# The feed-forward down projection as a two-by-two block product with seven block products, its sums made by VectorE

## What is computed

```python
gate = causal_dwconv(h @ w_gate, conv_w) + conv_b
return (jax.nn.silu(gate) * (h @ w_up)) @ w_down      # (256 x 5632) @ (5632 x 2048)
...
x = x + g2 * conv_ffn(h, ffn_w_gate[l], ffn_w_up[l], ffn_conv_w[l], ffn_conv_b[l], ffn_w_down[l])
```

## Time and profile before

| | |
|---|---|
| median of 3 runs | 3437.06 us (3432.53 to 3437.33) |
| the profiled execution's own time | 3433.15 us |
| its span, first to last instruction | 3431.5 us |
| mean granted TensorE clock | 0.913 |
| TensorE matmuls busy | 2862.7 us, 83% |
| VectorE busy | 1491.9 us, 43% |
| ScalarE busy | 453.9 us, 13% |
| HBM read | 918.41 MB, 270 GB/s over the span |

### The profile page before, as it was taken

One profiled execution on the slowest core, in us unless ns is written; L12 is line 12 of the kernel. 1 busy time (PEld: TensorE's weight loads), 2 busy tenths in 40 slices (PEclk: granted clock), 3 DMA queues, 4 the chain that ended last, 5 costly groups with the idle time before them and its releaser, 6 DMA issues.

```text
span 3431.5 us, 25630 instructions
## 1 busy us (share of the span) xinstructions
PE 2862.7 (83%) x9302; PEld 1698.2 (49%) x9302; DVE 1491.9 (43%) x2221; ACT 453.9 (13%) x1049; POOL 938.2 (27%) x713
## 2 busy tenths in 40 slices
PE   5999877989999999999999997677776666666666
PEld 3443656578888885444447746233332222222222
DVE  5665265122300000000205407665667776767765
ACT  1000233021010100000205501000010111000000
POOL 2111100000000000000002204655556566665563
PEclk9999978899999999999999998888898888888888
DMA  9999320346544444444631147999999999999998
GB/s 379 395 401 363 116 90 35 123 160 245 207 147 155 151 150 144 147 159 147 210 124 53 39 159 304 419 388 417 390 403 422 422 421 411 418 422 422 421 422 357
DMA packets 232376, 922.74 MB, mean 269 GB/s; under 512 B 17820, under 2 KB 37476, under 8 KB 160356
## 3 DMA queue, kind: packets, MB, share of 16 engines
q0 software_dynamic: 99840, 637.57, 45.3%
q1 hardware_dynamic: 132181, 283.96, 24.1%
q10 hardware_dynamic: 272, 0.13, 0.0%
HBM read 918.41 MB, written 8.44 MB: 270 GB/s over the span
## 4 chain that ended last, share of the span: by engine, by line
PE 56%; DMA 24%; DVE 10%; POOL 5%; issue 3%; ACT 2%; POOLq 0%; DVEq 0%; SPq 0%; ACTq 0%
PE ps L1278 18%; PE ps L966 11%; DMA arena<-in_peer_v,proj 11%; PE ps L1304 9%; PE ps L1515 6%; DMA proj<-in_peer_v,proj 4%; DMA proj<-in_peer_u,proj 4%; DMA ring<-in_w_in 3%; PE ps L1087 3%; DMA arena<-in_w_mod 2%; POOL arena L520 2%; PE ps L1492 2%; PE ps L1004 2%; POOL proj L520 1%; DVE proj L2122 1%
## 5 line engine op out<-in xcount | busy, mean ns | idle before, releaser
L1515 PE MATMUL ps<-proj,gates 128*128 128x512 f32 x992 | 574.2, 743 | 383.9 <-DMA proj<-in_peer_v,proj 272.3
L1278 PE MATMUL ps<-hT,ring 128*128 128x256 f32 x2816 | 608.2, 379 | 1.5 <-ACT hT L559 1.5
L1515 PEld LDWEIGHTS ps<-proj,gates 128*128 128x128 f32 x992 | 233.2, 243 | 721.4 <-issue 602.1
L1278 PEld LDWEIGHTS ps<-hT,ring 128*128 128x128 f32 x2816 | 535.0, 190 | 74.8 <-issue 2.2
L966 PE MATMUL ps<-ring,hT 128*128 128x512 f32 (+2 forms) x960 | 382.8, 559 | 8.0 <-DMA ring<-in_w_in 7.9
L2122 DVE CUSTOM_DVE_ANT_0 arena<-arena,yT 128x2048 f32<-128x2048 f32 x128 | 291.5, 2291 | 211.1 <-DMA arena<-in_peer_u,proj 210.6
L2122 DVE CUSTOM_DVE_ANT_0 proj<-proj,yT 128x2048 f32<-128x2048 f32 x128 | 292.1, 2292 | 121.5 <-DMA proj<-in_peer_u,proj 117.8
L1304 PE MATMUL ps<-ring,arena 128*128 128x512 f32 x704 | 304.1, 595 | 2.7 <-ACT arena L766 2.7
L520 POOL DMA_INDIRECT proj<-in_peer_u,proj x128 | 209.5, 1637 | 309.4 <-DVE proj L2115 146.0
L966 PEld LDWEIGHTS ps<-ring,hT 128*128 128x128 f32 x960 | 174.9, 193 | 212.7 <-issue 192.2
L1515 PE MATMUL ps<-arena,gates 128*128 128x512 f32 x512 | 235.6, 603 | 36.9 <-DMA arena<-in_peer_v,proj 36.7
(11 more groups left out here) (416 smaller groups left out, 2600.6 us busy)
## 6 DMA issues: line engine op xcount, KB each, us to landing
arena<-in_w_mod POOLq DMA_DIRECT2D x96, 1024.0 KB, 12.4
ring<-in_w_in SPq DMA_DIRECT2D x52, 1024.0 KB, 12.0
ring<-in_ffn_w_gate SPq DMA_DIRECT2D x44, 1024.0 KB, 5.0
ring<-in_ffn_w_up SPq DMA_DIRECT2D x44, 1024.0 KB, 5.1
ring<-in_ffn_w_down SPq DMA_DIRECT2D x44, 1024.0 KB, 4.8
ring<-in_w_out SPq DMA_DIRECT2D x32, 1024.0 KB, 5.2
ring<-in_peer_wq SPq DMA_DIRECT2D x16, 1024.0 KB, 16.5
ring<-in_w_in SPq DMA_DIRECT2D x16, 960.0 KB, 17.6
```

The lines of the kernel that those rows point to most:

```text
L1278: ins = pe.matmul(ps[:, 4 * m + f, 0:T], ring[:, s, k, P * f:P * (f + 1)], hT[:, KS * s + k, :], start=(s == 0 and k == 0), stop=(s == SLO ...
L1515: ins = pe.matmul(ps[:, 4 * t + b, :], diag[:, j, :], row_slots[n % ROWS][:, NB * b:NB * (b + 1)], start=(h == 0 and j == 0), stop=(h == H ...
```

## The change

The product A B of the activations A (256 x 5632) and the weights B (5632 x 2048) is cut in two by two blocks: the tokens in halves of 128, the inner dimension in halves of 22 tiles, the columns in halves of 1024. Each half of the columns is worked in two pieces, so that one pass (`half`) handles blocks of 512 columns: pass 0 the blocks 0 and 2, pass 1 the blocks 1 and 3. There are 44 steps, 22 in each pass. Step k of a pass takes tile k and tile 22 + k of the inner dimension and makes seven products P1 to P7 in seven banks, in place of eight:

- the left factors are A11, A12, A22 and four sums of activations, s1 to s4 (`left_sums`, on VectorE between the groups of the up projection; they are kept in `arena` and `yT`);
- the right factors are B11, B21, B22 and four differences of weights, made by VectorE for each step from the ring's slot (`right_sums`, into `t`, two buffers in `hT`);
- behind each pass ScalarE copies P1 out of PSUM and VectorE makes seven sums of the products (`parts`), and then multiplies by the gate and adds to `x` (`gated`). Those of pass 0 lie between the steps of pass 1.

The staging copies of ScalarE are gone. A slot is loaded by two transfers of 512 KB in rows of 2 KB, where it was one of 1 MB in rows of 8 KB. `in2` begins with the quarters of the width in the order 0, 2, 1, 3. All steps are written out, with no loop. The core of the diff:

```diff
-        wd = a["ffn_w_down"].rearrange("(j s p) n -> p j s n", s=SLOTS, p=P)
-        with sp.Fori(0, DOWN) as i:
-            for s in range(SLOTS):
-                sp.wait_ge(*at("unit_used", i * SLOTS + (BLK["down"] * SLOTS + s - SLOTS + 1)))
-                sp.dma_start(ring[:, s, :, :], wd[:, bass.ds(i, 1), s, :].rearrange("p o (k n) -> p (o k) n", n=NB)).then_inc(sem(f"slot{s}"), 16)
+        wd = a["ffn_w_down"].rearrange("(h j p) (e c n) -> p h j c e n", h=2, p=P, e=2, n=NB)
+        for step in range(DOWN_STEPS):
+            half, k = divmod(step, HALF_K)
...
+                sp.wait_ge(*down_used(step - SLOTS + 1))
+            for h in range(2):
+                sp.dma_start(ring[:, step % SLOTS, 2 * h:2 * h + 2, :], wd[:, h, k, half]).then_inc(sem(f"slot{step % SLOTS}"), 16)
...
-        for j in range(2):
-            act.copy(ffn["act"][:, j], act_store[:, 4 * j:4 * j + 4, :]).then_inc(sem("staged"), 1)
...
+        for half in range(2):
+            act.wait_ge(*down_used(HALF_K * (half + 1)))
+            act.copy(corner[:, 0], ps[:, DOWN_BANK[half]["P1"], :]).then_inc(sem("down_p1"), 1)
...
+        def down_step(step):
...
+            pe.wait_ge(*down_slot(step))
+            product("P1", act_of(k, 0), b[:, 0, :])
+            if first:
+                pe.wait_ge(*at("down_p1", 1))
+            product("P2", act_of(HALF_K + k, 0), b[:, 2, :])
...
+            if first:
+                pe.wait_ge(*down_part(0, 1))
+            product("P3", s_of["s4"][:, k, :], b[:, 3, :])
+            if first:
+                p4()
+            pe.wait_ge(*down_t(step, 1))
+            if first:
+                pe.wait_ge(*down_part(0, 3))
+            product("P5", s_of["s1"][:, k, :], t[:, 0, :])
...
+                if q == 0:
+                    pe.wait_ge(*at("x_done", 3))
+                    pe.wait_ge(*down_part(0, PARTS))
+                    pe.wait_ge(*at("down_p1", 2))
+                    raw_turn(2, IN2_ORDER[0], IN2_TURN[0])
+                    pe.wait_ge(*down_part(1, 2))
+                    raw_turn(2, IN2_ORDER[1], IN2_TURN[1])
+                    pe.wait_ge(*down_part(1, 6))
+                if q == 1:
+                    pe.wait_ge(*at("x_done", 5))
...
+            vec.tensor_tensor(s3, a11, a21, ALU.subtract)
+            link(vec.tensor_tensor(s1, a21, a22, ALU.add))
+            link(vec.tensor_tensor(s2, s1, a11, ALU.subtract))
+            link(vec.tensor_tensor(s4, a12, s2, ALU.subtract), name)
...
+            vec.wait_ge(*down_slot(step))
+            vec.wait_ge(*down_used(max(step - 1, 0)))
+            link(vec.tensor_tensor(t[:, 0, :], b[:, 1, :], b[:, 0, :], ALU.subtract), "down_sums", wait=False)
+            link(vec.tensor_tensor(t[:, 2, :], b[:, 3, :], b[:, 1, :], ALU.subtract), "down_sums")
+            link(vec.tensor_tensor(t[:, 1, :], b[:, 3, :], t[:, 0, :], ALU.subtract), "down_sums")
+            link(vec.tensor_tensor(t[:, 3, :], t[:, 1, :], b[:, 2, :], ALU.subtract), "down_sums", wait=False)
...
+            part_sum(1, 0, "P2")
+            part_sum(0, 0, "P6")
+            part_sum(3, 0, "P7")
+            part_sum(2, 0, "P5")
+            part_sum(2, 2, "P3")
+            part_sum(4, 3, "P5")
+            part_sum(3, 3, "P4", ALU.subtract)
```

More of the change, by code:

```diff
@@ L43 @@
 _b = 0
-for _n, _c in (("in1", 12), ("out1", 4), ("up", 22), ("down", 11), ("in2", 7), ("out2", 4), ("wq", 4)):
+for _n, _c in (("in1", 12), ("out1", 4), ("up", 22), ("down", 22), ("in2", 7), ("out2", 4), ("wq", 4)):
     BLK[_n] = _b
@@ L951, in raw_turn, with project @@
             ins.then_inc(sem("hT_turned"), 1)
-        def project(lhs, blk, ev, n, tail, by_vec=True, begin=None):
+        def project(lhs, blk, ev, n, tail, by_vec=True, begin=None, order=range(SLOTS)):
             def one(i, step, b, w, between=None):
@@ L1295, in _ @@
         pe.wait_ge(*at("up_free", 12))
[L1297 to L1313, removed]
+        def down_step(step):
+            half, k = divmod(step, HALF_K)
+            bank, b, t = DOWN_BANK[half], ring[:, step % SLOTS], t_of[:, step % 2]
+            first = half == 1 and k == 0
+            def product(name, lhs, rhs):
+                return pe.matmul(ps[:, bank[name], :], lhs, rhs, start=(k == 0), stop=(k == HALF_K - 1))
+            def p4():
+                pe.wait_ge(*down_t(step, 4))
+                if first:
+                    pe.wait_ge(*down_part(0, 2))
+                return product("P4", act_of(HALF_K + k, 1), t[:, 3, :])
+            pe.wait_ge(*down_slot(step))
[3 more added lines that the diff above has]
+            product("P2", act_of(HALF_K + k, 0), b[:, 2, :])
+            if step == 0:
+                pe.wait_ge(*at("down_sums", 1))
+            if first:
[4 more added lines that the diff above has]
+            pe.wait_ge(*down_t(step, 1))
+            if first:
+                pe.wait_ge(*down_part(0, 3))
+            product("P5", s_of["s1"][:, k, :], t[:, 0, :])
+            pe.wait_ge(*down_t(step, 2))
+            if first:
+                pe.wait_ge(*down_part(0, 5))
+            product("P7", s_of["s3"][:, k, :], t[:, 2, :])
+            pe.wait_ge(*down_t(step, 3))
+            if first:
+                pe.wait_ge(*down_part(0, 6))
+            ins = product("P6", s_of["s2"][:, k, :], t[:, 1, :])
+            if not first:
+                ins = p4()
+            ins.then_inc(sem("unit_used"), 2)
@@ L1315, in turn_kv @@
+        for step in range(DOWN_STEPS):
+            down_step(step)
         def turn_kv(i, bank):
@@ L1953, in _ @@
+        left_sums(10)
+        for step in range(2, DOWN_STEPS):
+            if step == HALF_K + 1:
+                parts(0)
+            right_sums(step)
+            if HALF_K < step <= HALF_K + 4:
+                gated(0, step - HALF_K - 1)
+        parts(1)
+        for n in range(4):
+            gated(1, n)
         norm(2, scaled=False)
```

91 lines of the change are left out of this document (62 added, 29 removed).

## The result

| | before | after |
|---|---|---|
| median | 3437.19 us (3432.53 to 3441.38, 4 runs) | 3394.18 us (3390.49 to 3396.95, 4 runs) |
| the profiled execution | 3433.15 us, span 3431.5 | 3396.95 us, span 3395.2 |

The changed kernel takes 43.0 us less, at a ratio of 0.9873 to the kernel before, with a 95% interval of [0.9861, 0.9885]. Forecast were 3393 us and 41.9 us less.

What follows compares the result with a forecast made beforehand. The prediction took TensorE alone to bound the down projection. Its terms, 37.8 + 1.1 + 1.7 + 1.8 - 0.45 = 41.9 us, came off 3435.0 us, the mean of four known times, giving 3393 us; range 3387 to 3408.

Steps and rivals of the forecast that it cites:

- Matmuls removed: In the down projection, one matmul of 0.858 us less in each of 44 steps: 37.8 us won.
- Start and clock: Down projection's start: TensorE begins 1.1 us earlier without the staging copy; a 1.6 us gap leaves its clock up, 1.7 us won.
- left sums: Between the up projection's groups, VectorE's 2.8 us a group lie in its idle time: cost 0.
- right sums: In each down projection step, VectorE's 2.8 us of 6.0 are done about 3.2 us before the next step: cost 0.
- waits: Between down projection matmuls, five waits a step, 220 in all: cost 0, bound 2.2 us.
- contention: In the down projection, VectorE reads the ring while TensorE does: cost 0, at worst 2.5 us.
- loads: Down weights come by two issues of 512 KB in rows of 2 KB, covered by the lead: cost 0.
- From pass 0 to pass 1: Step 22 takes over banks as they are emptied and ends at 6.45 us in place of 6.0: 0.45 us lost.
- Start of `in2`: First `in2` matmul 5.3 us behind the stage's last, before 7.1: 1.8 us won; upper end adds 2.1 if matmuls run warm.
- the price of a wait: Rivals: one wait a step delays a load 0.24 us, 3404 us (7%); each of 220 waits does, 3446 us (2%).
- the falling clock: Rival (2%): TensorE idles at every step and its clock drops mid-stage; with half the records at the lower level, 3525 us.
- the return of the gain in `in2`: Rival (4%): a 17.80 us transfer of `w_in` in the `in2` chain does not move along, up to 17.8 us return: 3411 us.

Runs made afterwards that it cites:

- the eighth product: The changed kernel with an eighth matmul in each step, whose result nobody reads: 3435.34 us, ratio 0.9988.
- the copy put back: The changed kernel with ScalarE's staging copy of 128 x 1024 put back ahead of the first step, its result not read: 3395.72 us, ratio 0.9866.
- the split loads: The kernel before, with each slot of the down weights loaded by two transfers of 512 KB in rows of 2 KB: 3436.58 us, ratio 0.9995.
- the doubled sums: The changed kernel with VectorE making each right sum twice, once into memory that nobody reads: 3399.76 us, ratio 0.9877.
- the kernel with one wait: The changed kernel with one wait for the fourth right sum ahead of P5 in place of four waits for one sum each: 3392.86 us, ratio 0.9859.
- the tripled sums: The changed kernel with VectorE making each right sum three times, the extra ones into memory that nobody reads: 3520.13 us, ratio 1.0226.
- the early start: The changed kernel with P2 and P3 of step 0 ahead of P1, so TensorE need not wait at the stage's start: 3395.04 us, ratio 0.9874.

## Why the prediction was right

It was right, and by the steps that it gave. That 3393 us came within 1.2 us of the median is in part luck: the 3435.0 us from which it subtracts lie 2.2 us under the median of the kernel before in the result, and the 41.9 us are 1.1 us short of the difference of the medians.

*Matmuls removed* (1): 37.8 us, and the eighth product gives back 37.8.

*Start and clock* (2, 3): the pause was 1.43 us, 0.2 less than worked out, since the hand-over from VectorE to TensorE took 0.1 us (VectorE's last multiplication ends at 1331.27, TensorE starts at 1331.37) in place of the 0.25 taken over from ScalarE. The clock stayed up, as taken, and the copy put back brings back both, 3.0 us. The prediction chose here between two rows far apart, 0.89 and 2.7 us, "by a little". The timeline of the kernel before has a nearer one in the last stage, right behind the one used, which kept the level with 1.46 us of idle time:

```profile
2525.65 3.67 PE L1515 MATMUL ps<-proj,gates 128*128 128x512 f32 x8 [1.46 <-DMA proj<-in_peer_v,proj]
```

*What was costed at nothing* (4 to 8): left sums, right sums, waits, contention and loads cost nothing. The page shows it for the left sums, and the right sums have the cover that was worked out. VectorE's timeline in the last ordinary steps of pass 0 and across its end (L2013 to L2016 are the right sums, L2022 the sums of the pass):

```profile
1457.89 0.69 DVE L2013 TENSOR_TENSOR hT<-ring 128x512 f32<-128x512 f32 x1 [3.26 <-PE ps L1320]
1458.50 0.68 DVE L2014 TENSOR_TENSOR hT<-ring 128x512 f32<-128x512 f32 x1
1459.22 0.69 DVE L2015 TENSOR_TENSOR hT<-ring,hT 128x512 f32<-128x512 f32 x1
...
1464.52 5.01 DVE L2022 TENSOR_TENSOR arena<-arena,ps 128x512 f32<-128x512 f32 x7 [3.88 <-ACT arena L789]
1469.57 0.69 DVE L2013 TENSOR_TENSOR hT<-ring 128x512 f32<-128x512 f32 x1
```

Between the steps it is idle for 3.26 us; 3.2 was forecast. The dense waits, the split loads and the doubled sums were each tried alone. Contention was not tried alone; what speaks against it is the interval, which has not grown with VectorE busy for 46 to 48% of the time.

*From pass 0 to pass 1* (9): TensorE's timeline of steps 21 (from 1457.62), 22 (from 1463.63) and 23 (from 1470.03):

```profile
1457.62 1.88 PE L1320 MATMUL ps<-ring,proj 128*128 128x512 f32 x4
...
1463.63 1.96 PE L1320 MATMUL ps<-ring,proj 128*128 128x512 f32 x4
...
1467.15 1.02 PE L1320 MATMUL ps<-hT,yT 128*128 128x512 f32 x2
1468.23 1.96 PE L1320 MATMUL ps<-hT,arena 128*128 128x512 f32 x4
1470.03 1.88 PE L1320 MATMUL ps<-ring,proj 128*128 128x512 f32 x4
```

Step 22 takes 6.40 us against 6.01, a loss of 0.39 where 0.45 was worked out. The break is where it was expected, ahead of P7, whose bank is the fifth to be emptied: P7 starts 1.08 us behind P5 (1467.15 to 1468.23), where 0.86 is the interval.

*Start of `in2`* (10): TensorE's timeline, which answers to the earlier trace rows:

```profile
1597.13 1.07 PE L967 MATMUL ps<-tab,x 128*128 128x128 f32 x8 [0.77 <-ACT arena L789]
1598.55 1.09 PE L967 MATMUL ps<-tab,x 128*128 128x128 f32 x8 [0.35 <-DVE arena L2022]
1601.44 7.13 PE L983 MATMUL ps<-ring,hT 128*128 128x512 f32 x16 [1.79 <-DVE arena L2022]
```

The first matmul comes 5.1 us behind the last of the stage; 5.3 was forecast. The one term that was missed is behind it: I took the 16 records to run as before, 9.01 us, with the clock down. They took 7.13. The saving of 1.9 us stood in the sum only as its upper end. So the gain is 42.4 + 1.9 = 44.3 us by the two traces, against the forecast 41.9; the two medians give 43.0 and 45.0.

The rivals are out: the price of a wait by the kernel with one wait, the falling clock by the 1.00 of the stage, and the return of the gain in `in2` by its next 80 records, which take 34.50 us in the traces of both kernels; the chain of the changed one has no transfer of `w_in` there. The 17.80 us of that transfer in the earlier trace rows were no waiting time to give back: TensorE idled for 0.23 us of it, ahead of 1696.55. The argument against the falling clock was weaker than it looked. The earlier trace rows has single pauses of 0.89 us, and with a pause of 0.5 to 1.1 us two or three times in each step the tripled sums did bring the clock down. What rules the rival out is that TensorE does not wait in ordinary steps.

## What to carry to other kernels

A stage whose chain is one engine alone can be shortened by arithmetic that lets an idle engine do part of it; the gain here was the count of removed instructions times their interval, with the helper's work for a step under the step and started early enough. That meant 2.8 us of sums in 6.0, two buffers, and a step's lead.

Look then at both ends of the stage. What the new arithmetic adds behind the last matmul (seven sums and four gated ones, 10.8 us) has to find work to lie beside. An order of the next stage that starts with what is long finished was worth 9.6 us here.

For effects of a few us, measure in the trace between two fixed points around the change. The end of the up projection scattered by 9 us from trace to trace of the same program, while the stretch behind it repeated within 0.1.

## What the runs showed that I had not expected

The clock is not given by the length of a pause alone. Ahead of `in2`, pauses of 0.8, 0.4 and 1.8 us with two groups of turns between them kept the full level in six traces of five kernels: the changed one (twice), the eighth product, the doubled sums, the one wait and the copy put back (first 16 records in 7.13 us). With the early start they lost it in one of two traces of the same program, taken on two chips (8.83 against 7.13), and with tripled sums too (8.72), where the stage ahead had pauses of its own. The kernel before, with pauses of 2.8 and 1.4 us there, lost it in all three traces, the one with the split loads among them (9.01, 9.02, 9.01). So with such pauses one trace does not show what they cost.

VectorE's sums that do not depend on each other start 0.61 us apart, those that wait for the one ahead 0.72 (1457.89, 1458.50, 1459.22). And VectorE, reading the ring for 46 to 48% of the time, did not lengthen TensorE's interval of 0.429 us by anything that the rows show (281 records in 120 us).
